# Column-tiled sample attention and a one-table softplus in a hybrid decoder step

## What is computed

```python
z = q @ k.T * SB_SCALE + bias            # one bias per head
log_fail = where(causal, log_sigmoid(-z), 0)     # = -softplus(z)
log_a = z + reverse_cumsum(log_fail)
a = exp(where(causal, log_a, -inf)); out = a @ v
```

## Time and profile before

| | |
|---|---|
| median of 3 runs | 5219.49 us (5214.43 to 5241.15) |
| profiled execution | 5217.44 us, span 5215.6 us |
| busy: PE / DVE / ACT / POOL | 2732.2 / 3676.9 / 1161.1 / 1502.4 us |
| prompt attention, groups 0, 1, 2 | 231 to 308, 968 to 1185, 2112 to 2408 us |
| sample attention | 2408 to 3125 us |
| the last 480 expert rows | 3703 to 5215 us |
| table loads, prompt lines 664 and 669 | 96 and 93 |
| table loads, sample lines 1303 and 1306 | 40 and 40 |

### The profile page before, as it was taken

The page is one execution under the profiler, slowest core; times in us unless marked ns, Lnnn a source line. Parts: engine busy times, 40 slices in busy tenths (PEclk is TensorE's granted clock), DMA queues, the critical chain, the costliest instruction groups (busy, mean ns, idle before and its releaser), DMA issues. The chain is left out here.

```text
span 5215.6 us, 35243 instructions
## 1 busy us (share of the span) xinstructions
PE 2732.2 (52%) x8368; PEld 1495.1 (29%) x8368; DVE 3676.9 (70%) x6451; ACT 1161.1 (22%) x1815; POOL 1502.4 (29%) x1385
## 2 busy tenths in 40 slices
PE   8678884457866983456898978977300000000000
PEld 6466642344533332343232323433200000000000
DVE  0111367895766888896454546877799989989988
ACT  0330101582211102695343431211000000000000
POOL 0000033232322343111111112323244444445544
PEclk9789996568978995677898988988655555555555
DMA  5234499778888998657889878989689899899898
GB/s 203 94 133 161 153 379 338 249 254 330 347 345 330 364 389 307 218 195 285 334 320 352 312 279 327 372 337 382 249 305 363 330 355 353 339 358 364 337 353 321
DMA packets 311553, 1579.54 MB, mean 303 GB/s; under 512 B 36407, under 2 KB 95851, under 8 KB 155630
## 3 DMA queue, kind: packets, MB, share of 16 engines
q0 software_dynamic: 158288, 1151.42, 58.3%
q1 hardware_dynamic: 122558, 377.48, 19.2%
q10 hardware_dynamic: 30560, 49.03, 2.5%
HBM read 1526.55 MB, written 50.99 MB: 302 GB/s over the span
## 5 line engine op out<-in xcount | busy, mean ns | idle before, releaser
L1566 POOL DMA_INDIRECT peer_row<-in_peer_uv,peer_staged x1088 | 1344.5, 1236 | 2966.8 <-DVE peer_y L1770 2777.1
L1754 DVE SCALAR_TENSOR_TENSOR peer_row<-peer_row,peer_x 128x1024 f32<-128x1024 f32 x1088 | 1326.5, 1219 | 279.7 <-DMA peer_row<-in_peer_uv,peer_staged 225.4
L1770 DVE SCALAR_TENSOR_TENSOR peer_y<-peer_row,peer_coef,peer_y 128x1024 f32<-128x1024 f32 x1088 | 1391.4, 1279 | 0.2
L1654 ACT ACTIVATE peer_coef<-peer_hid 128x4 f32<-128x4 f32 x272 | 55.8, 205 | 2303.5 <-DVE peer_row L1754 2302.1
L243 PE MATMUL pr_b<-pr_xT,pr_w 128*128 128x256 f32 (+2 forms) x1152 | 390.7, 503 | 106.5 <-DMA pr_xT<-in_xT 76.7
L814 PE MATMUL gs_gp<-gs_xT,gs_w 128*128 128x256 f32 (+2 forms) x1152 | 392.9, 495 | 52.1 <-DMA gs_w<-in_w_gate 47.9
L243 PEld LDWEIGHTS pr_b<-pr_xT,pr_w 128*128 128x128 f32 x1152 | 226.0, 197 | 269.8 <-issue 178.8
L814 PEld LDWEIGHTS gs_gp<-gs_xT,gs_w 128*128 128x128 f32 x1152 | 223.1, 194 | 210.4 <-issue 144.2
L1213 PE MATMUL sa_z<-sa_kc,sa_qpad 128*64 128x512 f32 x512 | 258.4, 664 | 32.5 <-DMA sa_kc<-in_cache_k 32.5
L824 PE MATMUL gs_bp<-gs_brT,gs_w 128*128 128x256 f32 (+2 forms) x768 | 265.7, 495 | 18.2 <-DMA gs_brT<-scratch_mT 13.3
L1003 PE MATMUL rt_b<-mg_zT,rt_w 128*128 128x256 f32 (+2 forms) x768 | 256.2, 498 | 31.9 <-DMA rt_w<-in_w_q 31.9
(11 more groups left out here) (199 smaller groups left out, 3682.8 us busy)
## 6 DMA issues: line engine op xcount, KB each, us to landing
sa_kc<-in_cache_k SPq DMA_DIRECT2D x128, 512.0 KB, 8.4
sa_vc<-in_cache_v SPq DMA_DIRECT2D x128, 512.0 KB, 7.4
pr_w<-in_w_in SPq DMA_DIRECT2D x27, 2048.0 KB, 11.0
gs_w<-in_w_gate SPq DMA_DIRECT2D x36, 1024.0 KB, 9.6
rt_w<-in_w_q SPq DMA_DIRECT2D x24, 1024.0 KB, 8.5
peer_row<-in_peer_uv,peer_staged POOLq DMA_INDIRECT x1088, 7.7
gs_w<-in_w_br SPq DMA_DIRECT2D x24, 512.0 KB, 5.3
gs_w<-in_w_br SPq DMA_DIRECT2D x12, 1024.0 KB, 7.8
```

Source lines behind the costliest of these rows:

```text
L1566: pool.indirect_dma_start(out=self.row[b][:], out_offset=None, in_=dr["peer_uv"], in_offset=bass.IndirectOffsetOnAxis(ap=self.staged[slot] ...
L1654: act.activation(self.coef[:, c], self.hid[:, c], ACT.Gelu_apprx_tanh).then_inc(self.gelued, 1)
L1754: v.scalar_tensor_tensor(out=self.row[b][:, 0:D], in0=self.row[b][:, 0:D], scalar=1.0, in1=self.x1[:], op0=ALU.mult, op1=ALU.mult, accum_o ...
L1770: v.scalar_tensor_tensor(out=self.y[:], in0=self.row[b][:, D:2 * D], scalar=self.coef[:, col:col + 1], in1=self.y[:], op0=ALU.mult, op1=AL ...
```

## The change

In the sample attention the eight heads are put on 128 rows: four strips j of 32 rows, each with two heads (hh = 0, 1) of 8 queries and 16 empty rows. A score product takes 32 columns of weights and writes 32 output rows, and the four strips are issued one after another, twice. The value products are 4 pages x 4 strips of 256 columns (the two heads of the strip) into a 128 x 256 bank. The gathering products and `sel` are replaced by two transposes of 128 columns; the mask is added by VectorE; `vn` has a buffer of its own; the bias is a column of 128 rows.

In both attentions softplus(z + b) is written as max(z + b, 0) + ln(1 + exp(-|z + b|)). VectorE makes `positive` = max(z + b, 0) (rectify) and -2 * positive + z (fold), ScalarE takes Exp with the bias and Ln(1 + .), and the scan adds both rows; CAP and the row of ones are gone. In the prompt rectify(k + 2) stands ahead of the scan of piece k, and fold(k + 2) behind its subtraction. A table set that has both Exp and Ln is loaded explicitly at the start of a stage and after each background step that used ScalarE (`beside`). The diff, cut to its core:

```diff
@@ -574,7 +575,7 @@
...
-                    pe.wait_ge(softened, 3 * (k - RING) + 3)
+                    pe.wait_ge(softened, 2 * (k - RING) + 2)
@@ -616,17 +617,22 @@
...
         def _(v):
-            v.memset(one[:], 1.0).then_inc(one_set, 1)
-            v.wait_ge(one_set, 1)
             v.wait_ge(const_loaded, 48)
 
-            def cap(k):
+            def rectify(k):
                 h, n = pieces[k][0], pieces[k][3]
                 v.wait_ge(scored, k + 1)
+                v.tensor_scalar(positive[k % RING][:, 0:n], z[k % RING][:, 0:n], bias[:, h:h + 1], 0.0,
+                                ALU.add, ALU.max).then_inc(rectified, 1)
+
+            def fold(k):
+
+                n = pieces[k][3]
+                v.wait_ge(rectified, k + 1)
                 if k >= RING:
                     v.wait_ge(turned, k - RING + 1)
-                v.tensor_scalar(soft[k % RING][:, 0:n], z[k % RING][:, 0:n], bias[:, h:h + 1], CAP,
-                                ALU.add, ALU.min).then_inc(capped, 1)
+                v.scalar_tensor_tensor(out=soft[k % RING][:, 0:n], in0=positive[k % RING][:, 0:n], scalar=-2.0,
+                                       in1=z[k % RING][:, 0:n], op0=ALU.mult, op1=ALU.add).then_inc(folded, 1)
 
@@ -634,22 +640,24 @@
...
                 b = bias[:, h:h + 1]
+                if k + 2 < N:
+                    rectify(k + 2)
                 v.wait_ge(logged, 2 * k + 2)
-                v.scalar_tensor_tensor(out=sf, in0=zz, scalar=b, in1=sf, op0=ALU.add,
-                                       op1=ALU.max).then_inc(softened, 1)
-                if k + 2 < N:
-                    cap(k + 2)
-                v.wait_ge(softened, 3 * k + 1)
-                v.tensor_tensor_scan(out=total[:, ::-1], data0=one[:].to_broadcast([P, n]), data1=sf[:, ::-1],
-                                     initial=0.0 if is_first else sums[(k - 1) % 2][:, 0:1], op0=ALU.mult,
+                if not is_first:
+                    v.wait_ge(softened, 2 * k - 1)
+                v.tensor_tensor_scan(out=total[:, ::-1], data0=positive[k % RING][:, 0:n][:, ::-1], data1=sf[:, ::-1],
+                                     initial=0.0 if is_first else sums[(k - 1) % 2][:, 0:1], op0=ALU.add,
                                      op1=ALU.add).then_inc(softened, 1)
                 bg.vector(v, "prompt", 2 * k, 2 * N)
-                v.wait_ge(softened, 3 * k + 2)
+                v.wait_ge(softened, 2 * k + 1)
                 v.scalar_tensor_tensor(out=sf, in0=zz, scalar=b, in1=total, op0=ALU.add,
                                        op1=ALU.subtract).then_inc(softened, 1)
-
-            cap(0)
-            cap(1)
+                if k + 2 < N:
+                    fold(k + 2)
+
+            for k in range(2):
+                rectify(k)
+                fold(k)
             for k in range(N):
@@ -657,15 +665,16 @@
...
             def soften(k):
-                sf = soft[k % RING][:, 0:pieces[k][3]]
-                act.wait_ge(capped, k + 1)
-                act.activation(sf, sf, ACT.Exp).then_inc(logged, 1)
+                h, n = pieces[k][0], pieces[k][3]
+                sf = soft[k % RING][:, 0:n]
+                act.wait_ge(folded, k + 1)
+                act.activation(sf, sf, ACT.Exp, bias=bias[:, h:h + 1]).then_inc(logged, 1)
                 act.wait_ge(logged, 2 * k + 1)
...
                 sf = soft[k % RING][:, 0:pieces[k][3]]
-                act.wait_ge(softened, 3 * k + 3)
+                act.wait_ge(softened, 2 * k + 2)
                 act.activation(sf, sf, ACT.Exp).then_inc(weighed, 1)
@@ -688,17 +697,23 @@
...
 
+            def beside(i):
+                if bg.scalar(act, "prompt", i, 2 * N):
+                    act.preload_act_table_set(EXP_AND_LN)
+
+            act.preload_act_table_set(EXP_AND_LN)
+            act.wait_ge(const_loaded, 48)
             soften(0)
...
                     soften(k + 1)
-                bg.scalar(act, "prompt", 2 * k, 2 * N)
+                beside(2 * k)
                 weigh(k)
...
                     keep(k - 2)
-                bg.scalar(act, "prompt", 2 * k + 1, 2 * N)
+                beside(2 * k + 1)
             copy(N - 1)
@@ -1045,45 +1060,48 @@
+    HH = 2
+    HJ = HEADS // HH
+    W = P // HJ
-        qpad = ph.sb("qpad", [P, HEADS * (R + NQ)])
+        qpad = ph.sb("qpad", [P, HJ, HH, W])
-        osb = ph.sb("osb", [R, HEADS * P])
-        vn = osb[0:NQ]
+        osb = ph.sb("osb", [P, HH * P])
+        vn = ph.sb("vn", [NQ, HEADS * P])
-        z = [ph.ps(f"z{i}", [R, CW]) for i in range(2)]
-        aT_ps = [ph.ps(f"aTp{i}", [P, CHUNK_PAGES * R]) for i in range(2)]
-        o_ps = ph.ps("o", [R, HEADS * P])
+        z = [ph.ps(f"z{i}", [P, CW]) for i in range(2)]
+        aT_ps = [ph.ps(f"aTp{i}", [P, CHUNK_PAGES * P]) for i in range(2)]
+        o_ps = ph.ps("o", [P, HH * P])
...
@@ -1169,38 +1187,39 @@
...
-                for h in range(HEADS):
-                    pe.matmul(fin_ps[0:R, 0:NQ], qpad[:, h * R:(h + 1) * R], kn[:, h, bass.ds(i * NQ, NQ)],
-                              start=h == 0, stop=False)
-                pes.done(pe.matmul(fin_ps[0:R, 0:NQ], ident[0:R, 0:R], negn[:], start=False, stop=True), "n_z")
+                for hh in range(HH):
+                    for j in range(HJ):
+                        last = pe.matmul(fin_ps[W * j:W * (j + 1), 0:NQ], qpad[:, j, hh, :],
+                                         know[:, HH * j + hh, :], start=hh == 0, stop=hh == HH - 1)
+                pes.done(last, "n_z")
...
-                        last = pe.transpose(aT_ps[1][0:NQ, 0:R], loga[1][:, 0:NQ], ident[0:R, 0:R])
+                        last = pe.transpose(aT_ps[1][0:NQ, 0:P], loga[1][:, 0:NQ], ident[:])
...
-                        for hf in range(2):
-                            last = pe.matmul(o_ps[:, hf * 512:(hf + 1) * 512], aT[1][0:NQ, 0:R],
-                                             vn[:, hf * 512:(hf + 1) * 512], start=True, stop=False)
+                        apart(pe, dr["unwaited"])
+                        for j in range(HJ):
+                            last = pe.matmul(o_ps[W * j:W * (j + 1), :], aT[1][0:NQ, W * j:W * (j + 1)],
+                                             vn[:, HH * P * j:HH * P * (j + 1)], start=True, stop=False)
...
-                        last = pe.transpose(aT_ps[s][:, k * R:(k + 1) * R], loga[s][:, k * P:(k + 1) * P],
-                                            ident[0:R, 0:R])
+                        last = pe.transpose(aT_ps[s][:, k * P:(k + 1) * P], loga[s][:, k * P:(k + 1) * P], ident[:])
...
-                        for hf in range(2):
-                            last = pe.matmul(o_ps[:, hf * 512:(hf + 1) * 512], aT[s][:, k * R:(k + 1) * R],
-                                             vc[s][:, k, hf * 512:(hf + 1) * 512], start=False,
+                        for j in range(HJ):
+                            last = pe.matmul(o_ps[W * j:W * (j + 1), :], aT[s][:, k * P + W * j:k * P + W * (j + 1)],
+                                             vc[s][:, k, HH * P * j:HH * P * (j + 1)], start=False,
@@ -1209,30 +1228,32 @@
...
-                    for h in range(HEADS):
-                        last = pe.matmul(z[s][:], qpad[:, h * R:(h + 1) * R], kc[s][:, :, h * P:(h + 1) * P],
-                                         start=h == 0, stop=h == HEADS - 1)
+                    for hh in range(HH):
+                        for j in range(HJ):
+                            h = HH * j + hh
+                            last = pe.matmul(z[s][W * j:W * (j + 1), :], qpad[:, j, hh, :],
+                                             kc[s][:, :, h * P:(h + 1) * P], start=hh == 0, stop=hh == HH - 1)
...
-                for h in range(HEADS):
-                    last = pe.matmul(fin_ps[:, 0:R], osb[:, h * P:(h + 1) * P], sel[:, h, :], start=h == 0,
-                                     stop=h == HEADS - 1)
+                for hh in range(HH):
+                    last = pe.transpose(fin_ps[:, hh * P:(hh + 1) * P], osb[:, hh * P:(hh + 1) * P], ident[:])
...
-            v.memset(one[:], 1.0).then_inc(cleared, 1)
...
-            v.wait_ge(cleared, 3)
-            v.wait_ge(const_loaded, 16 * 8)
+            v.wait_ge(cleared, 2)
+            v.wait_ge(const_loaded, 16 * 7)
...
-                v.tensor_copy(qpad[:].rearrange("p (h c) -> p h c", c=R + NQ)[:, :, 0:NQ],
-                              q[:, :, bass.ds(i * NQ, NQ)])
+                v.tensor_copy(know[:], kn[:, :, bass.ds(i * NQ, NQ)])
+                for hh in range(HH):
+                    v.tensor_copy(qpad[:, :, hh, hh * NQ:(hh + 1) * NQ],
+                                  q[:].rearrange("p (j hh) n -> p j hh n", hh=HH)[:, :, hh, bass.ds(i * NQ, NQ)])
@@ -1244,25 +1265,29 @@
...
+                pes.wait(v, i, "n_z")
+                dve.done(v.tensor_tensor(zn[:], fin_ps[:, 0:NQ], negn[:], op=ALU.add), "n_mask")
+                dve.wait(v, i, "n_mask")
...
```

(39 more changed lines are left out.)

## The result

The changed kernel takes 5047.9 us (median of 4 runs, 5038.1 to 5056.3) against 5217.0 us of the kernel before on the same chip: a ratio of 0.967, 95% interval 0.963 to 0.972. The prediction was 5109 us with a range of 5055 to 5200: the sign and the mechanism hold, but the time lies 7 us under the low end. The profiled execution took 5041.7 us (span 5040.0).

What follows compares the result with a forecast made beforehand. TensorE was taken to bound the sample stage, VectorE the prompts of groups 1 and 2. 5217.4 - 77 (sample stage) - 33 (softplus and one table set) = 5107, the median 2 us above: 5109 us, range 5055 to 5200.

Steps and rivals of the forecast that it cites:

- What bounds the kernel, and that the strips overlap: Sample stage: TensorE sets it, busy 610 of 717 us; four overlapping strips save 220 to 290 us of TensorE time.
- rival B: Sample stage: weight loads exposed on every pass, 163 us in the stage, total 5339 us, slower; chance 0.09.
- What is late next: Sample stage after tiling: DMA transfers become the bound at 640 us, ahead of VectorE's chain at 535; gain 77 us.
- the chain: Sample stage: VectorE's own work of 45.7 us per sequence plus remaining waits, 67 us per sequence, 535 us in all.
- 600 / 0.94 = 640: Sample stage: 231.6 MB at 386 GB/s take 600 us; divided by an assumed DMA share of 0.94, 640 us.
- 600 us at the very least: Sample stage: lower limit from 231.6 MB at the best 50 us window's 386 GB/s; gain there 117 us.
- Softplus and the table set: Prompt stages: softplus by rectify and fold with one table set gains 33 us, ends 5 and 50; VectorE's operations cost 0.
- Group 1's term: Group 1's prompt: 3 us gained from VectorE's waits for ScalarE, which were 2.0 us.
- the 49 of the floor: Group 0's prompt: TensorE's 37.3 us busy and the wait at the start give a floor near 46 + 3 us.
- rival C: Prompts of groups 1 and 2: VectorE waits 0.7 us per piece for scores, 56 us; total 5178 us; chance 0.08.
- A: Sample stage: strips don't overlap, TensorE stays the bound at 14.2 us a chunk; total 5176 us; chance 0.12.
- D: Both attentions: single table set isn't kept, loads remain; prompts gain 0, sample 5 us less, total 5147 us; chance 0.09.

## Why the prediction was right or wrong

**What bounds the kernel, and that the strips overlap: right.** TensorE set the sample stage, and the column tiling alone took 125 us out of it. The prediction put a chunk's products at 1.7 us for scores and 3.4 to 5.7 for values; at the full clock they take 1.91 and 1.93. The bound by 32 weight loads in a row (0.106 us each) was wrong: 32 loads and their passes fit into 1.93 us, 0.06 us each, so loads of different strips overlap each other too. At the lower level both take 3.64 us, which the prediction had not allowed for. The Trainium skill (TensorE: Matmul & The Clock Gate, Packing small matmuls) gives 2.38 times for three column strips; four measured 3.7 times here, against the kernel before. By rival B, weight loads out from under the products, the stage would have taken some 870 us; the sentence of the Trainium skill behind it (same page and section), that a weight load overlaps a running product only when the row group differs, is not borne out here: all four strips use all 128 rows, and in the stretch at 2711 us TensorE is busy with products for all of 1.90 us and with loads for 0.91 of it.

**What is late next: right in kind, mis-sized.** Of the 61 us between forecast and median, 47 lie in the sample stage (124.4 us gained, 77 forecast) and 8 or 9 in the prompts (41.5 and 33). The prediction named the DMA as the next bound, 640 us, and the chain behind it, 535 us. The half-page run puts the chain at 526 at most. The term that failed is 600 / 0.94 = 640; measured were 595.5 us. Its two factors measured:

- The rate. The 386 GB/s of the best 50 us window were moved at a share of 0.99, 390 at a share of one, and the window was the best of one cut only. Cut 6 us later, the trace of before has 402 GB/s, in a stage whose TensorE was busy 0.82 of the time:

```profile
2906.00:2956.00 50.00, 41.14 (x119) 14.73 (x120) 21.99 (x34) 18.12 (x26) 5.90 (x6) 0.90 1.01 402
```

 In the stage after, 50 us windows reach 412 at a share of 1.02:

```profile
2662.30:2712.30 50.00, 30.04 (x193) 10.68 (x197) 28.40 (x64) 15.21 (x29) 8.64 (x9) 0.62 1.02 412
```

- The share: 0.98, where 0.94 was taken for gaps around each sequence's change. The best windows show 1.02, so few such gaps are left.

With 390 / 0.98 = 398 GB/s at a share of one, 231.6 MB at 0.94 would be 619 us, 21 less than forecast; the share 0.98 takes another 23 to 25 off. So about half of the 45 us missed here is the rate and half the gaps. The end that was to be "600 us at the very least" was no bound: the full change and five other kernels with the same sample transfers went under it (595.5, 594.5, 593.3, 591.0, 587.4 and 587.2). A floor must come from the fastest stretch at any cut, and the low end of the range had been built on this one. With 412 GB/s the floor would have been 562 us and the low end about 5217 - 155 - 45, some 5020. The stated low end also took 45 us for the prompts, where its own end for them was 50.

**Softplus and the table set: right.** Scan 1286 to 1275 ns with the new operands: priced at 0, and it is 0, so a row in place of a broadcast costs nothing; that the recurrence sets the time was argued and not tested. The fold takes 687 ns where the maximum, with a per-row scalar, took 739; the exponential of 512 columns takes 721 ns where it took 630, and what is new in it is the per-row bias. Group 1's term (3 us) measured 2.5. Group 0 (20) gave 16.9: TensorE waits 25.4 us for the head loads, as in the earlier trace rows; the stage takes 61.1 us and not the 49 of the floor, and what sets the other 12 no run tested. **Group 2 was taken too low**: 10 against 22.1 in this profile and about 18 in the other kernels with the same prompt. The wait for the logarithm (12.5 us) went whole, not by four fifths, and VectorE's own busy time fell by 4.2 us, 3.2 of it at the fold. These make 16.7 us; of the rest of this profile's 22.1, 3.4 us lie behind VectorE's last operation in the stage. VectorE is busy 94% of group 2, as foreseen (93% and more), and 90% of group 1. The prediction kept a discount for rival C, VectorE waiting at the early rectify; no such cost shows in group 2 behind the stage's start.

**Rivals.** A and B fell with the 1.91 and 1.93 us, C with the place of its wait and the moved rectify, D with the count of the loads. The run without the explicit load shows what D would have cost, 40 us on the full change (5088 against 5048); the prediction had put 38 on it, of them 33 on the prompts, where the run had 47. The Trainium skill's drain with each table load (ScalarE: Activation LUTs, What ACT_TABLE_LOAD costs: 1.38 us beside the load) does not show either: in the prompt of group 2 with two sets ScalarE's idle time ahead of 95 loads is 1.7 us in all, and ahead of the logarithms that follow the first load of each pair 0.5 us.

**The rest.** The remaining 10 us of the 176 lie outside these four stages, whose neighbours have the same work; the stretch behind the sample stage varied between 2075 and 2097 us in kernels in which it is the same. This is scatter, not an effect.

## What to carry to other kernels

When a busy engine is relieved, read the next bound from the resource's best stretch at any cut, and split "bytes over rate" from "share": both move when the work that kept the queue waiting is gone. A product with few output rows is worth spreading over column strips, with neighbours in the queue going to different strips. And a stage in which one engine is busy 89% is not one in which another engine's work is free: what an added row costs must be measured, as it was between 1.7 and 2.9 us here by place.

## What the runs showed of the hardware

- Four column strips of 32 on the same 128 rows work together: 16 passes of 512 columns in 1.91 us instead of 7.08 at the full clock, and 32 passes of 256 columns, each with its own weights, in 1.93.
- The order in the queue counts: with eight value passes of a strip in a row the 32 passes take 4.59 us instead of 1.93, while four score passes in a row lose nothing (1.94 us).
- The DMA engines moved 412 GB/s over 50 us at a share of 1.02. With pages cut to half their columns (rows of 2 KB instead of 4) it was 313 / 0.86 = 364 GB/s at a share of one, against 390 / 0.98 = 398 with whole rows; one execution each.
- VectorE's scan takes 1275 ns for 512 columns, with a full row as its first operand and an addition, and 1286 with a broadcast and a multiplication.
